# Hybrid decoder on one core: the feed-forward block in two phases, gate and up for all chunks first, then down over all of K

## The reference, cut to what matters

```
h   = RMSNorm(x);  p = h @ w_in            # q, k, v, z, xBC, dt
x   = x + concat([attention, ssm]) @ w_out
h   = RMSNorm(x)
ff  = (silu(h @ w_gate) * (h @ w_up)) @ w_down     # D_FF = 5632
x   = x + ff
```

## Time and profile before

| | |
|---|---|
| median of three runs | 2186.34 us (2185.56 to 2186.9) |
| profiled execution, span | 2184.5 us |
| PE busy | 2165.0 us (99%) |
| DVE, ACT, POOL busy | 1272.9, 1004.1, 111.1 us |
| DMA, share of 16 engines | 55.9% in the weight queue, mean 179 GB/s |
| granted TensorE clock, mean | 0.997 |

### The profile page before, as it was taken

One profiled execution on the slowest core, in us unless ns is written; L12 is line 12 of the kernel. 1 busy time (PEld: TensorE's weight loads), 2 busy tenths in 40 slices (PEclk: granted clock), 3 DMA queues, 4 the chain that ended last, 5 costly groups with the idle time before them and its releaser, 6 DMA issues.

```text
span 2184.5 us, 29947 instructions
## 1 busy us (share of the span) xinstructions
PE 2165.0 (99%) x10150; PEld 1794.3 (82%) x10150; DVE 1272.9 (58%) x1542; ACT 1004.1 (46%) x1284; POOL 111.1 (5%) x159
## 2 busy tenths in 40 slices
PE   9999999999999999999999999999999999999998
PEld 7888888888888888888878887888888888888887
DVE  5866765455555555555567666555555555555555
ACT  5555654444444434444355556544444444344442
POOL 2023100000000000000000232000000000000000
PEclk9999999999999999999999999999999999999999
DMA  6554356666656556665545533565665555666654
GB/s 217 174 164 135 116 174 188 192 193 193 190 189 189 189 192 192 192 187 189 174 147 182 159 122 127 182 192 187 191 193 190 191 189 188 191 192 192 187 189 153
DMA packets 202813, 391.55 MB, mean 179 GB/s; under 512 B 12224, under 2 KB 12592, under 8 KB 202736
## 3 DMA queue, kind: packets, MB, share of 16 engines
q1 hardware_dynamic: 201952, 388.67, 55.9%
q0 software_dynamic: 784, 1.90, 0.3%
HBM read 388.43 MB, written 2.10 MB: 179 GB/s over the span
## 4 chain that ended last, share of the span: by engine, by line
PE 97%; ACT 1%; issue 1%; DVE 0%; SPq 0%; POOL 0%; DMA 0%; DVEq 0%; ACTq 0%; POOLq 0%
PE ps L458 91%; PE ps L467 3%; PE ps L557 1%; PE ps L506 0%; PE ps L621 0%; PE ps L620 0%; PE ps L593 0%; PE ps L594 0%; PE ps L619 0%; POOL ys L424 0%; PE ps L565 0%; PE ps L562 0%; PE ps L548 0%; ACT w_hi L770 0%; DMA vrows<-in_k_norm_w_dram 0%
## 5 line engine op out<-in xcount | busy, mean ns | idle before, releaser
L1003 DVE TENSOR_TENSOR w_lo<-raw,w_hi 128x1024 fp32r<-128x1024 f32 x736 | 905.7, 1232 | 739.0 <-ACT w_hi L985 544.4
L985 ACT CAST w_hi<-raw 128x1024 fp32r<-128x1024 f32 x480 | 506.7, 1056 | 739.4 <-PE ps L458 739.4
L458 PE MATMUL ps<-w_hi,h_hi 128*128 128x512 f32 x1984 | 624.0, 396 | 3.6 <-DVE h_lo L1012 3.5
L458 PE MATMUL ps<-w_hi,h_lo 128*128 128x512 f32 x1984 | 613.3, 390 | 0.0
L458 PE MATMUL ps<-w_lo,h_hi 128*128 128x512 f32 x1984 | 612.4, 390 | 0.0
L458 PEld LDWEIGHTS ps<-w_lo,h_hi 128*128 128x128 f32 x1984 | 373.3, 188 | 79.0
L458 PEld LDWEIGHTS ps<-w_hi,h_lo 128*128 128x128 f32 x1984 | 373.3, 188 | 78.8
L458 PEld LDWEIGHTS ps<-w_hi,h_hi 128*128 128x128 f32 x1984 | 366.5, 188 | 75.1 <-DVE w_lo L1003 4.4
L770 ACT CAST w_hi<-raw 128x1024 fp32r<-128x1024 f32 x256 | 269.9, 1055 | 199.9 <-PE ps L458 193.5
L458 PE MATMUL ps<-w_hi,m_hi 128*128 128x512 f32 x960 | 297.2, 391 | 2.6 <-DVE m_lo L1194 2.6
L458 PE MATMUL ps<-w_hi,m_lo 128*128 128x512 f32 x960 | 295.8, 389 | 0.0
(11 more groups left out here) (181 smaller groups left out, 852.5 us busy)
## 6 DMA issues: line engine op xcount, KB each, us to landing
raw<-in_w_gate_dram SPq DMA_DIRECT2D x176, 512.0 KB, 3.5
raw<-in_w_up_dram SPq DMA_DIRECT2D x176, 512.0 KB, 3.5
raw<-in_w_down_dram SPq DMA_DIRECT2D x176, 512.0 KB, 4.3
raw<-in_w_in_dram SPq DMA_DIRECT2D x144, 512.0 KB, 3.4
raw<-in_w_out_dram SPq DMA_DIRECT2D x64, 512.0 KB, 4.2
out_dram<-xr SPq DMA_DIRECT2D x4, 512.0 KB, 2.8
xr<-in_x_dram POOLq DMA_DIRECT2D x3, 512.0 KB, 6.7
xr<-in_x_dram SPq DMA_DIRECT2D x1, 512.0 KB, 4.4
```

The costliest lines, as they stand in the source:

```text
L458: done = nc.tensor.matmul(ps[:, bank + t, :], lhs[:, rows + k, t * P:(t + 1) * P], w[:, slot, k, :], start=(first and k == 0 and w is w_hi ...
L985: nc.scalar.copy(w_hi[:, s, :, :], raw[:, s, :, :]).then_inc(hi_split, 1)
L1003: v_.tensor_tensor(w_lo[:, slot, :, :], raw[:, slot, :, :], w_hi[:, slot, :, :].bitcast(F32), ALU.subtract).then_inc(lo_split, 1)
```

## The change

The feed-forward block becomes two phases. In the first, for each chunk c, PE does gate c and up c; the hidden values of chunk c - 1 are turned on PE after the third gate pair, as before, and written to `f_hi` and `f_lo`, which hold all 44 K tiles. In the second, each of the four blocks of 512 output columns is accumulated in PSUM over all 22 pairs of K and then added to x once (`add_down`). The factor `rs` moves from `up_evacuate` to `add_down`. Chunk 10 is turned after the third pair of the first down block.

To make room, `f_hi` and `f_lo` share their memory with `m_hi` and `m_lo` and with the buffers of attention and the scan, which are dead by then. Every `Fori` is gone: layers, chunks and SP's loads are written out, and each wait is on a constant. The work at the border of the layers moves into the second phase of layer 0: the small loads on SP go ahead of the last gate and up chunk, `vrows` is turned after the first down pair, and blocks 0 to 2 of the new x are turned, split and squared during down blocks 1 to 3. Block 3 is turned after pair 1 of layer 1. Stores of output blocks 0 to 2 are issued between the last weight loads.

```diff
-    P_LOOP = P_FF + 2 * PPG
-    DOWN = DCH * CT // 2
-    PER_FF = 2 * PPG + DOWN
-    P_LAST = P_LOOP + (FCH - 1) * PER_FF
...
+    FT = FF // P
+    PER_FF = 2 * PPG
+    P_DOWN = P_FF + FCH * PER_FF
+    DOWN = FT // 2
+    PAIRS = P_DOWN + DCH * DOWN
+    ALL = DEPTH * PAIRS
...
+        at_hi = 229344 - 2 * FT * TILE
+        at_lo = at_hi + FT * TILE
+        m_hi = f_hi = nc.alloc_sbuf_tensor_at("f_hi", [P, FT, TOK], F32R, offset=at_hi)
+        m_lo = f_lo = nc.alloc_sbuf_tensor_at("f_lo", [P, FT, TOK], F32R, offset=at_lo)
...
+                elif p < P_DOWN:
+                    c, q = (p - P_FF) // PER_FF, (p - P_FF) % PER_FF
+                    w, r, col = (w_gate, w_up)[q // PPG], 2 * (q % PPG), c * N
+                else:
+                    n, q = (p - P_DOWN) // DOWN, (p - P_DOWN) % DOWN
+                    w, r, col = w_down, 2 * q, n * N
+                return w[one, r * P:(r + 2) * P, col:col + N]
...
+                for p in range(PAIRS):
+                    load_pair(p % RING, layer * PAIRS + p, source(layer, p))
+                    if layer == 0 and p == 1:
+                        load_rows(0)
+                    if layer + 1 < DEPTH and p == P_DOWN - PER_FF:
+                        load_rows(layer + 1)
+                    if layer == DEPTH - 1 and p >= P_DOWN + DOWN and (p - P_DOWN) % DOWN == 8:
+                        store((p - P_DOWN) // DOWN - 1)
...
-                with pe.Fori(1, FCH) as c:
-                    first = base + c * PER_FF + (P_LOOP - PER_FF)
-                    evac = layer * EV_DVE + c * DCH + DCH
-                    pe.wait_ge(dve_evac, evac - 1)
-                    pe.wait_ge(act_evac, layer * EV_ACT + c + G_IN)
+                    if c == 0:
+                        pe.wait_ge(mixed_added, layer * DCH + DCH)
+                    else:
+                        pe.wait_ge(ff_ready, layer * FCH + c)
                     for q in range(PPG):
-                        products(q % RING, first + q, 2 * q, 2, h_hi, h_lo, q == 0, q == PPG - 1)
-                        if q == 2:
-                            turn_ff(4, layer * FCH + c)
-                    pe.wait_ge(dve_evac, evac)
-                    for q in range(PPG):
-                        products(q % RING, first + (PPG + q), 2 * q, 0, h_hi, h_lo, q == 0, q == PPG - 1)
+                        products(q % RING, base + (P_FF + c * PER_FF + PPG + q), 2 * q, up_bank(layer, c), h_hi, h_lo,
+                                 q == 0, q == PPG - 1)
+
+                for n in range(DCH):
+                    if n == 0:
+                        pe.wait_ge(gate_silu, layer * FCH + FCH)
+                    elif n == 1:
+                        pe.wait_ge(ff_ready, layer * FCH + FCH)
+                    else:
+                        pe.wait_ge(down_added, layer * DCH + (n - 1))
                     for q in range(DOWN):
-                        n = q // 2
-                        if q == 0:
-                            pe.wait_ge(act_evac, layer * EV_ACT + c + (G_IN + 1))
-                            pe.wait_ge(ff_lo, layer * 2 * FCH + 2 * c)
-                        elif q == 2:
-                            pe.wait_ge(ff_ready, layer * FCH + c + 1)
-                        elif q % 2 == 0:
-                            pe.wait_ge(dve_evac, evac + (n - 1))
-                        products(q % RING, first + (2 * PPG + q), 2 * (q % 2), 2 * ((n + 1) % 2), m_hi, m_lo,
-                                 q % 2 == 0, q % 2 == 1)
-                turn_ff(4, layer * FCH + FCH)
-                for q in range(DOWN):
-                    n = q // 2
-                    if q < 2:
-                        pe.wait_ge(ff_lo, layer * 2 * FCH + (2 * FCH - 1 + q))
-                    if q % 2 == 0:
-                        pe.wait_ge(dve_evac, layer * EV_DVE + (EV_DVE - 1 + n))
-                    products(q % RING, base + (P_LAST + q), 2 * (q % 2), 2 * ((n + 1) % 2), m_hi, m_lo,
-                             q % 2 == 0, q % 2 == 1)
+                        if n == 0 and q % 2 == 0:
+                            pe.wait_ge(ff_lo, layer * 2 * FCH + 2 * (q // 2 + 1))
+                        products(q % RING if n % 2 == 0 else (q + 2) % RING, base + (P_DOWN + n * DOWN + q), 2 * q,
+                                 down_bank(layer, n), f_hi, f_lo, q == 0, q == DOWN - 1)
+                        if n == 0 and q == 2:
+                            turn_ff(layer, FCH - 1)
+                        if layer + 1 < DEPTH and n == 0 and q == 0:
+                            turn_vecs(layer + 1)
+                        if layer + 1 < DEPTH and n and q == 1:
+                            if n == 2:
+                                pe.wait_ge(vec_ready, layer + 2)
+                            turn_x(layer + 1, 0, n - 1)
...
+                    if layer + 1 < DEPTH and p == P_DOWN + 1:
+                        act.wait_ge(vec_psum, layer + 2)
+                        own.done(nc.scalar.copy(vecs[:, :], ps[:, 6, 0:VROWS]))
+                        nc.scalar.mul(qw[:, :], vecs[:, V_Q:V_Q + 1], HEAD ** -0.5).then_inc(vec_ready, 1)
+                    if layer + 1 < DEPTH and p > P_DOWN + DOWN:
+                        n, q = (p - P_DOWN) // DOWN - 1, (p - P_DOWN) % DOWN
+                        if q == 1:
+                            x_hi(layer + 1, 0, n)
+                        if q == 2:
+                            x_chunk_squares(layer + 1, 0, n)
...
+            def add_down(layer, n):
+
+                dve.wait_ge(pair_used, layer * PAIRS + (P_DOWN + (n + 1) * DOWN + RING))
                 for t in range(T):
...
-                    last = v_.scalar_tensor_tensor(stage[:, 1, t, :], ps[:, t, :], rs[:, t:t + 1], stage[:, 0, t, :],
-                                                   ALU.mult, ALU.mult)
+                    v = xr[:, t, n * N:(n + 1) * N]
+                    last = v_.scalar_tensor_tensor(v, ps[:, down_bank(layer, n) + t, :], rs[:, t:t + 1], v,
+                                                   ALU.mult, ALU.add)
+                last.then_inc(down_added, 1)
+
...
+                if c:
+                    dve.wait_ge(ffT_psum, layer * 2 * FCH + 2 * c)
+                for t in range(T):
+                    last = v_.tensor_tensor(stage[:, 1, t, :], ps[:, up_bank(layer, c) + t, :], stage[:, 0, t, :],
+                                            ALU.mult)
                 last.then_inc(ff_ready, 1)
...
+                    if p == P_DOWN + 3:
+                        ff_low(layer, FCH - 1)
+                    if p >= P_DOWN:
+                        n, q = (p - P_DOWN) // DOWN, (p - P_DOWN) % DOWN
+                        if q == DOWN - 1:
+                            add_down(layer, n)
+                        if layer + 1 < DEPTH and n and q == 1:
+                            x_lo(layer + 1, 0, n - 1)
```

More of the change, by code:

```diff
@@ new lines, in _ @@
+            for layer in range(DEPTH):
+                for p in range(PAIRS):
[6 more added lines that the diff above has]
+                        store((p - P_DOWN) // DOWN - 1)
@@ L303, in _ @@
+            store(DCH - 1)
             sp.wait_ge(stored, DCH * 16)
@@ L307, in _ @@
         def _(pool):
[L308 removed]
+            own = Steps(pool, pool_step)
             def once(ins, n=[0]):
@@ L351, in _ @@
             pool.memset(numbers[:, 7:8], 0.0).then_inc(const_ready, 1)
-            with pool.Fori(0, DEPTH) as layer:
-                one = bass.ds(layer, 1)
+            for layer in range(DEPTH):
+                one = slice(layer, layer + 1)
                 for dst, src in ((dtb, dt_bias), (alog, a_log), (dskip, d_skip), (sink, sinks)):
@@ L762, in _, with split @@
         @block.scalar
         def _(act):
-            own = Steps(act, act_step, ACT_STEPS)
-            def split_hi(layer, slot, pair, turn):
-                act.wait_ge(raw_landed[slot], layer * (16 * PAIRS // RING) + turn * 16)
+            own = Steps(act, act_step)
+            def split(pair):
+                slot = pair % RING
+                act.wait_ge(raw_landed[slot], 16 * (pair // RING + 1))
                 act.wait_ge(pair_used, pair + 1)
                 nc.scalar.copy(w_hi[:, slot, :, :], raw[:, slot, :, :]).then_inc(hi_split, 1)
-            def split(layer, p):
-                split_hi(layer, p % RING, layer * PAIRS + p, p // RING + 1)
@@ L793, in squares @@
                 else:
-                    own.done(layer, ins)
+                    own.done(ins)
             def x_square(layer, i):
@@ L990, in _ @@
-                ff_high(layer * 2 * FCH + 2 * FCH - 1)
-                for p in range(P_LAST + LEAD, PAIRS):
-                    split(layer, p)
-            own.check()
+                        x_chunk_squares(layer, 1, (p - 82) // 8)
+                    if P_FF <= p < P_DOWN:
+                        c, q = (p - P_FF) // PER_FF, (p - P_FF) % PER_FF
+                        if q == PPG - 1:
+                            silu_gate(layer, c)
+                        if c and q == 3:
```

(11 more changed lines are left out.)

421 lines of the change are left out of this document (202 added, 219 removed).

## The result

| | before | after |
|---|---|---|
| median (runs) | 2186.11 us (4) | 2196.41 us (4), 2196.32 to 2196.58 |
| ratio | | 1.0048, 95% interval 1.0034 to 1.0063 |
| span of the profiled execution | 2184.5 us | 2194.8 us |
| granted clock, mean | 0.997 | 0.999 |

What follows compares the result with a forecast made beforehand. PE, busy 99% of the span, was taken as the bound, with gains only in its holes: -3.0 - 6.5 - 0.7 + 0.1 = -10.1 us on 2184.5, plus 1.84 from span to median: 2176.2 us; 80% range 2171.5 to 2181.

Steps and rivals of the forecast that it cites:

- The pairs and the matmuls: Whole kernel: number of pairs, matmul shapes and turns stay as before, 264 down pairs a layer in both; term 0.
- Tail: Chunk 10's turn in each layer: 17 pairs now precede its first reader, so PE's wait goes; -3.0 us in all.
- Border: Between layers 0 and 1: turns move into down, so the `h_lo` hole and the half-speed pair behind it go; -6.5 us.
- The branch: PE's inner loop: the skill's fetch rule would gain 67 us more; set aside, as starts across the branch are 0.45 us apart.
- Start: First 20 us, SP's loads: constants remove register instructions; between 0 and 2.7 us gained, taken as -0.7 us.
- Additions on DVE: Feed-forward: 160 fewer additions to x, 109 us less DVE work, hidden by PE; term 0.
- End: Ahead of the last store: two additions with a factor (747 ns) replace two without (684 ns); +0.1 us.
- The border does not close: Rival, chance 0.08: layer 1 waits again for block 3's `h_lo` or first splits, clock falls; 2182.7 us, no measurable change.
- More goes than the holes I count: Rival, chance 0.08: constants also shorten the gaps ending attention, and the start reaches its bound; 2171.2 us.
- Loads of down: Rival, chance 0.04: second phase bound by 88 `w_down` pair loads in a row; 37 us more, 2213 us.
- Longer code: Written-out loops: term 0; as a rival, chance 0.04, four instruction-fetch stalls of 3.71 us give 2191 us.

Runs made afterwards that it cites:

- the kernel 96 bytes lower: The changed kernel with `f_hi` and `f_lo` moved down by 96 bytes, so both start at a multiple of 128: 2175.94 us, ratio 0.9956 to the kernel before.

## Why the prediction was wrong, step by step

**The step that failed** is "The pairs and the matmuls", "Term: 0". It counted pairs, tiles, shapes and turns, and took the rate from one iteration of before. Its ground was "A tile of the activations is stationary in both, with the same shapes". The shapes were the same and the addresses weren't, and the term is +20.5 us: 2880 matmuls by 7.1 ns. The new addresses stand in the diff, `229344 - 2 * FT * TILE`; I read them as a matter of room. The trace of before couldn't give the price, since all its stationary operands on the long stretches begin at multiples of 128. But it gave no ground for 0 either: a place in memory that no row shows should have had a bound on both sides, as the start had. The forecast did name the sign by which to see it: "I would be wrong if starts of down matmuls were not 227 ns apart". They are 234. The failure is in having no chance and no price for it; none of the four rivals was about PE's own rate.

**The sum of the rest** held: with the address mended the kernel takes 2175.94, forecast 2176.2. Agreement to 0.3 us is in part luck: the kernel before alone had medians of 2185.1 to 2186.5 us in the sets of runs, and the terms below are off by more than that.

- *Tail, -3.0.* The mechanism is right: 0.79 us behind the turn. Undone alone it costs 2.4 us.
- *Border, -6.5.* The size is right, by the rows' distance 6.47. The cause is not. I took the hole as the price of the turns and of the chain over ACT and DVE that follows them. Of 6.47 only 1.71 come with the turns and the order of the splits. 4.76 come from DVE's loop branch, 1.80 us by itself, which lengthened a hole of 1.5 us to 3.5, and the clock fell only behind the longer one. The forecast came out since the change removed all of it at once.
- *The branch.* The prediction put the rule on fetches aside by PE's inner loop, whose branch takes nothing. In the built program a round of that loop is 331 instructions, and DVE's layer loop is 796. PE's layer loop is longer still, 2543, and nothing is seen in PE's work either: from the last down matmuls before the branch to `vrows`' turn behind it (1092.98) are 0.46 us, the usual distance of two:

```profile
1092.52 0.62 PE L458 MATMUL ps<-w_lo,m_hi 128*128 128x512 f32 x2
```

  But PE's sequencer was held there. Asked for their source lines, the trace of before has these rows for the branch of the layer loop (L644) and of the inner loop (L728): count, then shortest, median and longest in ns, first and last start in us. The shortest ones are those at a loop's end, which are not taken.

```profile
L644 PEldq COMPARE_BRANCH  x2: 74/1826/3578, 1089.0 to 2175.9; - x2
L728 PEldq COMPARE_BRANCH  x20: 76/210/252, 469.1 to 2151.7; - x20
```

  The branch back over the whole layer starts at 1089.0 and takes 3.58 us. It costs nothing because the matmuls that stand before it in the program, the last 17 of them at 227 ns each, keep PE busy until 1092.98; the next instruction of the sequencer stands at 1092.66, just in time. The same branch on ACT (648 instructions) is followed by the next instruction after 2.83 us (1082.37 to 1085.19), on SP (309) after 3.58 (1073.32 to 1076.90), and on POOL, whose layer loop has only 100 instructions, after 0.26 (373.25 to 373.51). So it held four engines for 2.8 to 3.6 us, and only on DVE did a part of it reach PE. The inner loops' branches take 0.21 to 0.25 us on PE, and on ACT the next instruction follows after 0.16 to 0.17.

  The Trainium skill (Runtime: NRT & Kernel Launch, section Instruction fetch mechanics) ties the fetch to a target outside the pages held. The trace agrees at the layer loops of PE, DVE, ACT and SP (2.8 to 3.6 us), and the short rounds of the inner loops on PE and ACT show no such stall (0.25 us at most). From what length on an engine stalls, no run here shows: SP does at 309 instructions, PE's inner loop of 331 does not. I had tested the rule on one branch of one engine, by PE's matmuls and not by its sequencer, and dropped it for all.
- *Start, -0.7.* Not settled. The issue of the last small load moved from 7.00 to 5.54 us, as the register pieces went, but the load then took 4.32 us instead of 3.71:

```profile
5.54 4.32 DMA vrows<-in_k_norm_w_dram
```

  So the end that said "they land at the same moment" holds for half of it. The second pair starts at 17.27 here, at 18.12 in the kernel 96 bytes lower and at 18.30 before: single executions, which differ by as much as the term.
- *Additions on DVE, 0.* Right: DVE is busy 97 us less (109 foretold) and PE gains nothing by it.
- *End, +0.1.* The last two additions take 1.41 us instead of 1.28.
- *The border does not close.* False: no wait stands at pair 0 or 6 of layer 1.
- *More goes than the holes I count.* False: in the aligned kernel PE is missing for 1.38 us at the end of attention in layer 0 (236 to 282 us), instead of 1.47.
- *Loads of down.* The rival is false: PE never waits for `w_lo`, and down goes at 226.7 ns with 88 pairs of `w_down` in a row. `w_down` lands in 3.6 us instead of 4.3.
- *Longer code.* No cost was seen. The instruction queue moved 1.31 MB instead of 0.69.

**Open:** why one misplaced tile in three costs more than a third of the whole; why a streamed operand at 64 bytes costs less than at 32; the start's share. Of the 4.76 us, 2.0 are the shorter hole and the rest is the pair that no longer runs at half speed; that is read from rows, and the two weren't tried apart.

## What to carry to other kernels

When a change gives a buffer an address by hand, or any new buffer moves those behind it, compare the first byte of every TensorE operand modulo 128 before and after; in a kernel that is bound by TensorE this is a term of the sum. Check the rate by the distance between starts, for neither the busy share nor the mean length of a record shows it. And when the view says that an engine waited for something that had long been ready, look in the chain for "issue" and a loop's line: here a branch back over the body of a layer held the engine's next instruction for 2.8 to 3.6 us. It costs as much of that as is not covered by work issued before it, even on an engine that is half idle, if TensorE waits for that engine there.

## What the hardware showed that was not expected

- A 128x512 fp32r matmul with a new stationary tile each time starts every 227 ns if both operands begin at a multiple of 128 bytes in the partition, and every 232.3 to 234.3 ns if the stationary one is 4 to 96 bytes past. bf16 at the same shape: 215.8 ns with the stationary operand at 0, 32, 64 and 96 bytes.
- The weight load's record stays at 188 ns in both cases.
- The branch back over a layer's body held the next instruction for 3.00 us on VectorE (796 instructions), 2.83 us on ScalarE (648), 3.58 us on SyncE (309) and 3.6 us on TensorE (2543), where 17 matmuls that stood before it hid all of it; GpSimd's, over 100 instructions, for 0.26 us. On VectorE 1.80 us showed. The branch over a round of TensorE's inner loop (331) takes 0.21 to 0.25 us.
- The granted clock fell to 0.50 behind a hole of 3.52 us in TensorE's work and not behind one of 1.52.
